# Banded attention in a fused decoder kernel: scores on two array halves, issued one place earlier, four q/k/v buffers

## The reference, cut to what matters

```
q = rope(rmsnorm(q)) * 64 ** -0.5 ;  k = rope(rmsnorm(k))
for g in 3 groups, 8 heads of 64:              # query t sees keys t, t-dil, ... (n_rel + 1 of them)
    s = q @ k.T on blocks of 128 queries and the block itself and the one before; -inf outside the band
    m = max(s); p = exp(s - m); l = sum(p); acc = p @ v        # all f32
o = sum_g acc_g * exp(m_g - max m) / sum_g l_g * exp(m_g - max m)
sample: s[b, j, h] = sum_d q[b, h, d] * kv[b, j, h, d]         # 211 rows a sample
```

## Time and profile before

| | |
|---|---|
| time, median of 3 runs | 3432.28 us (3430.13 to 3432.78) |
| profiled execution, first to last instruction | 3431.7 us |
| mean granted TensorE clock | 0.981 of full |
| PE busy, share of the span | 96% |
| DVE busy | 48% |
| ACT busy | 26% |

### The profile page before, as it was taken

The page is one execution under the profiler, slowest core; times in us unless marked ns, Lnnn a source line. Parts: engine busy times, 40 slices in busy tenths (PEclk is TensorE's granted clock), DMA queues, the critical chain, the costliest instruction groups (busy, mean ns, idle before and its releaser), DMA issues.

```text
span 3431.7 us, 57622 instructions
## 1 busy us (share of the span) xinstructions
PE 3302.9 (96%) x21956; PEld 3141.1 (92%) x21956; DVE 1647.8 (48%) x3356; ACT 878.4 (26%) x2294; POOL 112.3 (3%) x191
## 2 busy tenths in 40 slices
PE   7999998879999999999999999899999999999999
PEld 6999998856999999999999999867787999999999
DVE  7755648765633443344512212077666633443343
ACT  4433434542311111112211121133333311111110
POOL 0000000000000000000000000011111000000000
PEclk9999999988999999999999999999999999999999
DMA  4222225356511111111222222375654111111111
GB/s 148 95 77 92 77 81 175 120 154 256 196 49 37 49 51 47 37 50 61 75 91 83 95 95 83 103 235 191 196 177 135 38 49 37 39 59 49 37 37 49
DMA packets 166095, 326.32 MB, mean 95 GB/s; under 512 B 20209, under 2 KB 99777, under 8 KB 149881
## 3 DMA queue, kind: packets, MB, share of 16 engines
q1 hardware_dynamic: 148232, 195.33, 17.1%
q0 software_dynamic: 17712, 128.98, 10.7%
HBM read 250.28 MB, written 101.76 MB: 103 GB/s over the span
## 4 chain that ended last, share of the span: by engine, by line
PE 90%; DVE 6%; issue 1%; DMA 1%; ACT 1%; SPq 1%; DVEq 0%; ACTq 0%; PEldq 0%
PE ps L801 79%; PE ps L1045 2%; PE ps L1037 2%; PE ps L874 2%; PE ps L1029 1%; PE ps L900 1%; PE ps L1026 1%; DVE un L1095 1%; DVE hL L1086 1%; DVE al L1171 1%; PE ps L886 1%; DVE rt L1089 1%; PE ps L785 0%; PE ps L1012 0%; PE ps L1051 0%
## 5 line engine op out<-in xcount | busy, mean ns | idle before, releaser
L801 PE MATMUL ps<-hH,wH 128*128 128x344 f32 x2880 | 923.3, 321 | 15.7 <-DVE hL L1086 12.0
L801 PE MATMUL ps<-hH,wL 128*128 128x344 f32 x2880 | 921.6, 320 | 0.0
L801 PE MATMUL ps<-hL,wH 128*128 128x344 f32 x2880 | 920.7, 320 | 0.0
L801 PEld LDWEIGHTS ps<-hH,wH 128*128 128x128 f32 x2880 | 543.8, 189 | 18.8 <-issue 16.2
L801 PE MATMUL ps<-wH,hH 128*128 128x256 f32 x1872 | 529.5, 283 | 16.4 <-DVE qn L1136 7.1
L801 PEld LDWEIGHTS ps<-hH,wL 128*128 128x128 f32 x2880 | 543.1, 189 | 0.0
L801 PEld LDWEIGHTS ps<-hL,wH 128*128 128x128 f32 x2880 | 542.2, 188 | 0.0
L801 PE MATMUL ps<-wH,hL 128*128 128x256 f32 x1872 | 528.5, 282 | 0.0
L801 PE MATMUL ps<-wL,hH 128*128 128x256 f32 x1872 | 527.3, 282 | 0.0
L1080 DVE TENSOR_TENSOR wL<-raw,wH 128x2048 fp32r<-128x2048 f32 x123 | 281.3, 2287 | 507.4 <-ACT wH L557 507.4
L557 ACT ACTIVATE wH<-raw 128x2048 fp32r<-128x2048 f32 x123 | 233.1, 1912 | 706.8 <-PE ps L801 702.2
(11 more groups left out here) (167 smaller groups left out, 3882.6 us busy)
## 6 DMA issues: line engine op xcount, KB each, us to landing
raw<-in_w POOLq DMA_DIRECT2D x123, 1024.0 KB, 5.1
qkv_rows<-ot SPq DMA_DIRECT2D x144, 128.0 KB, 1.7
zS<-in_state_in SPq DMA_DIRECT2D x32, 512.0 KB, 4.9
ret_s<-zS SPq DMA_DIRECT2D x32, 512.0 KB, 6.0
kv_s<-in_cache SPq DMA_DIRECT2D x2, 8160.0 KB
qkv<-qkv_rows SPq DMA_DIRECT2D x48, 256.0 KB, 3.6
g_cols<-rw SPq DMA_DIRECT2D x48, 172.0 KB, 1.9
v_rows<-rw SPq DMA_DIRECT2D x64, 128.0 KB, 1.9
```

The costliest lines, as they stand in the source:

```text
L801: mm = pe.matmul(out, lhs[k][a], rhs[k][b], start=(k == 0 and q == 0), stop=(k == n - 1 and q == 2))
```

## The change

The scores contract over the 64 rows of a head alone: heads 0 to 3 in rows 0 to 63, heads 4 to 7 in rows 64 to 127, issued alternately (`HEAD_ORDER`). The turned q has four columns of 128 instead of eight, with nothing zeroed, and ACT copies all of it. PE issues `scores(a+1)` directly behind `turn(a+1)`, ahead of all four `turn_p` of unit a; `turn` waits also for the copy of q before, and `values` for the copy of the next q. Masks and maxima go in two halves (heads 0, 1, 4, 5 and 2, 3, 6, 7), a maximum in two reductions a half. ACT's order becomes four exponentials, q copy, two exponentials, a turned copy, two exponentials, a turned copy. The multiplies of the sample scores go to POOL, between two of its weight loads; the sums stay on DVE, at the end of the step. The q/k/v tiles have four buffers; SP loads v three and q/k four units ahead, behind the store of the accumulator. All 24 steps are written out, with no loops. `oH` and `oL` move to a later place in memory to make room.

```diff
+QS = 4
+HEAD_ORDER = (0, 4, 1, 5, 2, 6, 3, 7)
+TURN_ORDER = (0, 2, 1, 3)
+EXP_ORDER = (0, 1, 4, 5, 2, 3, 6, 7)
-    aq = sb("aq", [P, H, P], scope=B2)
+    aq = sb("aq", [P, 4, P], scope=B2)
-    qkv = sb("qkv", [P, 2, 3, AW], scope=B2)
+    qkv = sb("qkv", [P, QS, 3, AW], scope=B2)
...
@@ pool
+            load(mixing, 0)
+            load(mixing, 1)
+            for b in range(NS):
+                k = b % 2
+                pool.wait_ge(b_loaded[k], 16 * 8 * (b // 2 + 1))
+                for tl, n in ((0, P), (1, 83)):
+                    pool.tensor_tensor(bK[0:n, k, tl, :], bK[0:n, k, tl, :], bQ[0:n, k, tl, :], ALU.mult).then_inc(b_prod, 1)
+            load(mixing, 2)
...
@@ sync, for a in range(AU)
-                if a + 2 < AU:
-                    sp.wait_ge(q_turned, a + 1)
-                    at_load(a + 2, (0, 1), aqk_loaded)
-                if 1 <= a < AU - 1:
-                    sp.wait_ge(pv_done, a + 1)
-                    at_load(a + 1, (2,), av_loaded)
                 sp.wait_ge(acc_ready, a + 1)
...
+                if 1 <= a and a + QS - 1 < AU:
+                    at_load(a + QS - 1, (2,), av_loaded)
+                if a + QS < AU:
+                    at_load(a + QS, (0, 1), aqk_loaded)
...
@@ scalar
+            for a in range(AU):
+                act.wait_ge(m_ready, 2 * a + 1)
+                exps(a, EXP_ORDER[0:4])
                 if a + 1 < AU:
+                    queries(a + 1)
+                act.wait_ge(m_ready, 2 * a + 2)
+                exps(a, EXP_ORDER[4:6])
+                turned_odd(a, 1)
+                exps(a, EXP_ORDER[6:8])
+                turned_odd(a, 3)
...
@@ tensor, scores
-                for x in range(H):
+                for n, x in enumerate(HEAD_ORDER):
+                    rows = slice(x // 4 * DH, (x // 4 + 1) * DH)
                     for hf in ((0, 1) if AT_PREV[f] else (1,)):
...
-                                       aq[:, x, :], ak[:, (f + 1 + hf) % 2, x % 4, :], start=True, stop=True)
+                                       aq[rows, x % 4, :], ak[rows, (f + 1 + hf) % 2, x % 4, :], start=True, stop=True)
...
@@ tensor, steps
-                    turn(a + 1, i)
-                turn_p(a, i, 0)
-                turn_p(a, i, 1)
-                if a + 1 < AU:
-                    scores(a + 1, i)
-                turn_p(a, i, 2)
-                turn_p(a, i, 3)
-                values(a, i)
...
+            for a in range(AU):
+                if a + 1 < AU:
+                    turn(a + 1)
+                    scores(a + 1)
+                for n in range(4):
+                    turn_p(a, n)
+                values(a)
...
@@ vector
+            for a in range(AU):
                 if a + 1 < AU:
+                    keys(a + 1)
+                    masked(a + 1, 0)
+                turned_even(a, 0)
+                if a + 1 < AU:
+                    masked(a + 1, 1)
+                turned_even(a, 2)
+                if a + 1 < AU:
+                    maxima(a + 1, 0)
+                    maxima(a + 1, 1)
                 if a < NS:
+                    sample_scores(a)
+                dve.wait_ge(pv_done, a + 1)
                 dve.tensor_copy(al[:, a % 2, :, 0:DH], ps[:, 0, :].rearrange("p (x d) -> p x d", x=H)).then_inc(acc_ready, 1)
```

More of the change, by code:

```diff
@@ L316, in _ @@
             first = U_RO // SLOTS + 1
-            with pool.Fori(1, first) as r:
+            mixing = U_WO // SLOTS + 1
+            with pool.Fori(1, mixing) as r:
+                for s in range(SLOTS):
+                    load(r, s)
+            load(mixing, 0)
[6 more added lines that the diff above has]
+            load(mixing, 2)
+            with pool.Fori(mixing + 1, first) as r:
                 for s in range(SLOTS):
@@ L401, in _ @@
                 sp.wait_ge(stored[b], 16 * ((G - 1) * QKV_J // NB + 1))
-            for a in range(2):
+            for a in range(QS):
                 at_load(a, (0, 1), aqk_loaded)
@@ L624, in _, with queries, exps @@
                             act.activation(ot[:, b, :], ps[:, b, 0:HC], ACT.Copy).then_inc(drained[b], 1)
[L627 to L635, removed]
+            def queries(f):
+                act.wait_ge(q_turned, f + 1)
+                act.activation(aq[:, :, :], ps[:, 0, :].rearrange("p (c t) -> p c t", c=4), ACT.Copy).then_inc(aq_ready, 1)
+            def exps(f, xs):
+                for x in xs:
                     w_ = sc[:, f % 2, x, (0 if AT_PREV[f] else P):2 * P]
@@ L638, in exps, with turned_odd @@
                                    accum_out=al[:, f % 2, x, DH + 1:DH + 2]).then_inc(p_ready, 1)
[L640 to L665 removed]
+            def turned_odd(a, n):
+                q = TURN_ORDER[n]
+                act.wait_ge(p_turned, 4 * a + n + 1)
+                src = ps[:, 7, :].rearrange("p (x h t) -> p x h t", x=2, h=2)
+                if AT_PREV[a]:
+                    act.activation(pt[:, 2 * q:2 * q + 2, :, :], src, ACT.Copy).then_inc(pt_ready2, 1)
+                else:
+                    act.activation(pt[:, 2 * q:2 * q + 2, 1, :], src[:, :, 1, :], ACT.Copy).then_inc(pt_ready2, 1)
+            act.wait_ge(table_loaded, 32)
+            queries(0)
+            for a in range(AU):
+                act.wait_ge(m_ready, 2 * a + 1)
+                exps(a, EXP_ORDER[0:4])
+                if a + 1 < AU:
+                    queries(a + 1)
[4 more added lines that the diff above has]
+                turned_odd(a, 3)
             act.wait_ge(b_step, 2)
@@ L1174, in turned_p, with maxima @@
-            def turned_p(a, i, q):
-                dve.wait_ge(p_turned, i * 8 + (4 * a + q + 1))
+            def maxima(f, half):
+                k, w0 = f % 2, 0 if AT_PREV[f] else P
+                if half == 0:
+                    dve.wait_ge(acc_stored[k], 16 + 16 * sum(AT_PIECES[k:f:2]))
+                dve.wait_ge(s_masked, 4 * f + 2 * half + 2)
+                for par in range(2):
+                    x = slice(4 * par + 2 * half, 4 * par + 2 * half + 2)
+                    mx = dve.tensor_reduce(al[:, k, x, DH:DH + 1], sc[:, k, x, w0:2 * P], AX.X, ALU.max, negate=True)
+                mx.then_inc(m_ready, 1)
@@ L1207, in _, with sample_scores @@
-            dve.wait_ge(job_done, J_WO)
-            dve.memset(aq[:, :, :], 0.0).then_inc(aq_zeroed, 1)
-            dve.wait_ge(table_loaded, 32)
-            dve.wait_ge(aq_zeroed, 1)
-            keys(0, 0)
-            masked(0, 0)
-            maxima(0, 0)
-            for first, n, turns in AT_RUNS:
-                if turns == 1:
-                    for a in range(first, first + n):
-                        at_step(a, 0)
-                else:
-                    with dve.Fori(0, turns) as i:
-                        for a in range(first, first + n):
-                            at_step(a, i)
+            def sample_scores(b):
+                for tl, n, done in ((0, P, b_red), (1, 83, b_scored)):
+                    dve.wait_ge(b_prod, 2 * b + tl + 1)
+                    dve.tensor_reduce(bS[0:n, tl, b, :], bK[0:n, b % 2, tl, :].rearrange("p (h d) -> p h d", h=H), AX.X, ALU.add)\
+                        .then_inc(done, 1)
@@ new lines, in _ @@
+            dve.wait_ge(table_loaded, 32)
+            keys(0)
+            for half in range(2):
+                masked(0, half)
+                maxima(0, half)
+            for a in range(AU):
+                if a + 1 < AU:
+                    keys(a + 1)
[4 more added lines that the diff above has]
+                turned_even(a, 2)
+                if a + 1 < AU:
+                    maxima(a + 1, 0)
+                    maxima(a + 1, 1)
+                if a < NS:
+                    sample_scores(a)
+                dve.wait_ge(pv_done, a + 1)
+                dve.tensor_copy(al[:, a % 2, :, 0:DH], ps[:, 0, :].rearrange("p (x d) -> p x d", x=H)).then_inc(acc_ready, 1)
```

118 lines of the change are left out of this document (41 added, 77 removed).

## The result

The changed kernel takes 3436.49 us (median of 20 runs, 3433.95 to 3442.3), the kernel before beside it 3432.53 us (20 runs). The medians differ by 4 us, and the ratio of the runs is 1.0014, 95% interval [1.0007, 1.002]: 4 to 5 us slower, inside the 0.2% that was called no change, and near the 3435 us of the rival in which both array halves work fully at once. The sum of the prediction, 3445 us, lies 8.5 us above it.

What follows compares the result with a forecast made beforehand. The prediction took PE's chain of waits between accumulator copies to bound most steps, DVE last in narrow-to-wide ones. Steps of 217.0 against 201.5 us (+15.5), less 2.6 in the last step, gave +12.9, or 3445 us; range 3428 to 3467.

Steps and rivals of the forecast that it cites:

- the rival in which both array halves work fully at once: Scores at 1.84 us wide and 0.92 narrow; steps sum 206.5, +2.4 us in all, 3435, no change; chance 0.25.
- The chain: Wide step between accumulator copies: `al` to scores 2.23 us, values at S + 3.33, then 3.72 to `al`; S + 9.28.
- S: Score time of a step on PE: taken as 2.6 us wide and 1.2 narrow, from partial overlap of the halves.
- slower by over 0.2%: Whole-kernel outcome with chance 0.64: partial overlap 0.36, no overlap 0.22 and clock 0.06 together.
- lower bound: Score time with two halves perfectly at once: 1.84 us wide and 0.92 narrow.
- The rival of the clock: PE's granted clock falls every second step: 11 x 1.5 = 17 us on top of the sum, 3462; chance 0.06.
- The last step: From `al(22)` to the end of the steps: 4.7 us in place of 7.33, -2.6.
- `al(0)`: First accumulator copy: left where it is, with 2 us of doubt.
- POOL's pair of multiplies: A sample's two multiplies on POOL: 1.5 us each, 3 us a sample, counted as costing zero.
- The hand-offs from `al` to the q copy: Faster rival: written-out steps shrink eight hand-offs a step; at 0.12 us each -9 us, 3423; chance 0.11.

Runs made afterwards that it cites:

- Experiment 2: Changed kernel with the scores issued again behind the first two groups of probability transposes; 3421.76 us, ratio 0.9965 to the kernel before.
- experiment 1: Changed kernel with ACT's last two exponentials of a unit moved ahead of its first turned copy; 3436.1 us, ratio 1.0004 to the kernel before.
- experiment 3: Changed kernel with heads in order 0 to 7, four in one half and then four in the other; 3479.54 us, ratio 1.015 to the kernel before.
- experiment 6: Changed kernel with a sample's sums moved on DVE to the next step, behind the copy of k; ratio 1.0008 to the kernel before.
- experiment 9: Changed kernel with three buffers for the q/k/v tiles in place of four; ratio 1.0023 to the kernel before.
- experiment 4: Changed kernel with the sample's two multiplies back from POOL on DVE, ahead of the sums; ratio 1.0062 to the kernel before.
- experiment 8: Changed kernel with ACT's last two exponentials ahead of its first turned copy and sample sums in the next step; 3428.24 us, ratio 0.9986.
- experiment 10: Changed kernel with DVE's first turned copy ahead of the first masks and sample sums in the next step; ratio 1.0075 to the kernel before.

## Why the prediction came out as it did

**The chain was right.** `al` to scores was put at 2.23 us and took 2.15; scores to values in a wide step at S + 3.33, which is 5.27 us with the measured S of 1.94, and it took 5.33; values to `al` at 3.72, and it took 562.18 - 558.46 = 3.72. PE waits for ACT's q copy in nearly every step (15.1 us) and for the exponentials (11.5 us), as said, and waits for tiles are gone. Experiment 2 shows that the place of the scores is what costs, experiments 1 and 3 that exponentials and score time lie in that chain, experiment 6 that DVE does not set the sample steps.

The number was less right than the range makes it look. The sum gave 3445 us, and slower by over 0.2% had the most weight (0.64); measured is no change, which had 0.25. The time lies in the range because the range reaches down to the rival of full overlap.

**The score time was mis-sized.** This is the term of the sum that failed. The forecast took 2.6 and 1.2 us, from the thought that a block of four instructions in one half overlaps only at its edge. Measured by issue it is 32 x 0.061 = 1.94 and 16 x 0.059 = 0.94, against a lower bound of 1.84 and 0.92: four instructions in a row in one half do not spoil the overlap. With the lower bound the prediction gave steps of 11.12, 10.20, 9.25 and 7.40; measured are 11.21, 10.20, 8.95 and 7.35. So the rival of halves fully at once is what happened, within 0.3 us in every kind of step, and its +2.4 us stands beside +4.0 measured. That the two totals are so near is partly luck, as the ends below show. The Trainium skill, TensorEngine Tiling (Array Packing), section Key Properties, says that different tiles can load and multiply in parallel; the 0.061 us agree, and experiment 3 adds that they must alternate for it. The same section of the Trainium skill says that a change of the tiling mode drains the engine. From the first score to the first transpose it is 555.21 - 553.13 = 2.08 us against 1.94 of issue, so no more than 0.14 us of a drain shows here.

**The rival of the clock was right in kind, not in number.** Two steps fell, not its eleven: step 1 took 14.01 us in place of 11.21, step 13 took 11.19 in place of 10.20. Windows around the start of step 1, its q transposes and its scores:

```profile
536.00:540.00 4.00, 1.52 (x8) 1.16 (x10) 1.88 (x3) 1.35 (x6) 2.78 (x3) 0.73 0.36 105
540.00:544.00 4.00, 4.00 (x35) 3.78 (x34) 1.29 (x2) 0.44 (x2) 0.00 (x0) 0.50 0.85 292
```

```profile
537.79 1.04 PE L869 MATMUL ps<-ident,qkv 128*128 128x128 f32 x4 [2.78 <-DVE al L1207]
...
539.52 3.94 PE L881 MATMUL ps<-ak,aq 64*128 64x128 f32 x32 [0.69 <-ACT aq L643]
```

PE was busy for 1.52 of 4 us, waiting 2.78 us for `al(0)`, and the next 4 us run at 0.50 (experiment 6 takes that wait away, and with it the fall). These two falls, 2.8 + 1.0 us, are the difference between the full overlap's 206.5 us and the 209.33 measured, less about 1 us that the narrow-to-wide steps gave back.

**The ends.** The last step gained 3.1 us where 2.6 were forecast. But in experiments 6 and 9, which end with the same instructions, it takes 6.1 us, as its value products run at the lower clock there (experiment 6):

```profile
741.78 3.52 PE L910 MATMUL ps<-qkv,pt 128*128 128x64 f32 x16
```

So about 1.8 us of that gain hang on the clock. `al(0)` was left where it was, with 2 us of doubt, and came 2.25 us earlier. POOL's pair of multiplies was put at 3 us and takes 2.50; it is hidden but for step 0, where DVE waits 0.48 us for it. The hand-offs from `al` to the q copy did not shrink: they take 1.50 us where the prediction read 1.44, so nothing came of the written-out steps there.

**What lies behind the stage.** `al(23)` is 2.5 us later, but the profiled execution 6.4 us longer; 3.6 us of that lie between `al(23)` and the output projection. That stretch takes 59.9 us in the changed kernel and 60.0 in experiment 2, and 55.2 to 58.7 us in the kernel before and the other experiments, with no tie to an edit (55.7 in experiment 6, with the same PE steps as the changed kernel). DVE's work in it is the same 43.2 us before and after. Its end shows the larger part of the difference: the 64-row matmuls of the sample and the first of the projection, after and before.

```profile
808.06 1.88 PE L949 MATMUL ps<-bE,bA 64*128 64x8 f32 x8 [0.83 <-DVE bA L1276]
...
810.45 0.66 PE L809 MATMUL ps<-oH,wH 128*128 128x344 f32 x1 [0.51 <-DVE oL L1278]
```

```profile
802.81 1.05 PE L951 MATMUL ps<-bE,bA 64*128 64x8 f32 x8 [0.83 <-DVE bA L1290]
...
804.38 0.42 PE L801 MATMUL ps<-oH,wH 128*128 128x344 f32 x1 [0.51 <-DVE oL L1292]
```

After the change the last part of the stretch, from DVE's last full copy on, takes 6.17 us at a granted clock of 0.50 (804.28 to 810.45); before, it takes 3.60 us at 1.00 (800.78 to 804.38). That is 2.6 of the 3.6 us. Experiment 2 has the same 0.66 us at the projection's start, the others 0.42 or 0.43. Why the clock stayed low longer in these two stays open, and so does the rest. The profiled execution of the changed kernel also lies 3.3 us above the median of its runs (3439.78 us). So the 4 us measured are not to be read as the sum of the steps.

## What to carry to other kernels

Before an instruction group is issued earlier, list what it was standing behind: here the eight transposes that it overtook were the cover for a copy of q and the feed of the next engine, and 26 us of saved matmul time met 32 us of new waits (28 net of the old ones that went). The orders of the engines belong together: the same reordering of DVE cost 21 us with one order of PE and gained 18 us with the other. And when a chain is nearly dense, count a short wait of TensorE at more than its length, since the work right behind it may run at the lower clock.

## What the runs showed of the hardware

- Two groups of 64-row f32 matmuls that alternate between the array's halves issue every 0.059 to 0.061 us, half of the 0.115 us over 128 rows, though up to four in a row are in one half. One half after the other, they take 0.095 to 0.104 us.
- In every step of these traces in which TensorE waited 1.2 to 1.6 us and then 0.69 us one or two matmul groups later, the granted clock was 0.50 for several us behind it (experiments 1, 4, 8, 9 and 10). With 1.03 or 1.04 us ahead of the 0.69 this came in 7 of 20 steps (step 13 of the changed kernel, not its steps 9, 11 and 15), and in experiment 3 twice with only 0.43 us ahead (steps 3 and 12). Steps 2 to 6 of the changed kernel kept 1.00 with 0.43, 0.69, 0.44 and 0.60 us of waits spread over 11.2 us. So these waits alone do not settle when the clock falls.
- A POOL multiply of 128x512 takes 1.25 us (2.50 for two), less than twice the 0.76 us of its 128x256 addition.
